# Twelve upward tile pairs by seven products, in groups of three, where ten stood in couples

## What is computed

```python
def conv_ffn(h, w_up, conv_w, w_down):
    gu = causal_dwconv(h @ w_up, conv_w)
    g, u = jnp.split(gu, 2, axis=-1)
    return (jax.nn.silu(g) * u) @ w_down
```

## Time and profile before

| | us |
|---|---|
| median of 3 runs | 1209.61 (1208.76 to 1210.14) |
| the profiled execution | 1209.19 |
| its span, first to last instruction | 1207.4 |

### The profile page before, as it was taken

How to read it: one execution, slowest core, us unless ns; L and a number is a source line. 1 busy time by engine, 2 the same in 40 slices (tenths; PEclk the granted TensorE clock), 3 DMA queues, 4 the chain that set the end, 5 groups by cost and what they waited for, 6 DMA issues and landing times.

```text
span 1207.4 us, 19455 instructions
## 1 busy us (share of the span) xinstructions
PE 1194.9 (99%) x7027; PEld 997.9 (83%) x7027; DVE 754.0 (62%) x1366; ACT 649.4 (54%) x1259; POOL 734.6 (61%) x566
## 2 busy tenths in 40 slices
PE   9999999999999999999999999999999999999997
PEld 7987777777888899988797777778999998898886
DVE  6655426756646777646597646436888886966224
ACT  6365535676645344455644666456666664333543
POOL 6773232353359776856384557548877776986842
PEclk9999999999999999999999999999999999999999
DMA  7332222122223333363242123343333334434332
GB/s 247 105 89 84 62 62 62 53 66 76 70 62 96 93 100 96 104 186 110 55 119 62 45 70 100 93 149 93 91 98 104 103 100 112 159 97 118 109 88 70
DMA packets 63016, 116.51 MB, mean 96 GB/s; under 512 B 6920, under 2 KB 11528, under 8 KB 62408
## 3 DMA queue, kind: packets, MB, share of 16 engines
q1 hardware_dynamic: 62776, 115.25, 33.1%
q10 hardware_dynamic: 144, 0.00, 0.0%
HBM read 110.97 MB, written 4.26 MB: 95 GB/s over the span
## 4 chain that ended last, share of the span: by engine, by line
PE 81%; DVE 11%; issue 3%; ACT 2%; POOL 1%; DMA 1%; SPq 0%; DVEq 0%; ACTq 0%; POOLq 0%
PE pb L1190 18%; PE pb L1191 18%; PE pb L1193 18%; PE pb L1252 3%; PE pb L1254 3%; PE pb L1253 3%; DVE t8s L2218 2%; PE pb L1408 2%; DVE cv L2125 2%; PE pb L1261 2%; PE pb L1384 2%; PE pb L1351 1%; PE pb L1322 1%; PE pb L1324 1%; PE pb L1323 1%
## 5 line engine op out<-in xcount | busy, mean ns | idle before, releaser
L2892 POOL TENSOR_TENSOR wlo<-raw,whi 128x512 fp32r<-128x512 f32 (+2 forms) x374 | 505.3, 1369 | 327.2 <-ACT whi L1617 323.1
L1190 PE MATMUL pb<-HH,whi 128*128 128x512 f32 x696 | 282.6, 406 | 0.0
L1617 ACT ACTIVATE whi<-raw 128x512 fp32r<-128x512 f32 (+3 forms) x373 | 221.4, 615 | 107.2 <-PE pb L1193 54.8
L1191 PE MATMUL pb<-HL,whi 128*128 128x512 f32 x696 | 275.3, 395 | 0.0
L1193 PE MATMUL pb<-HH,wlo 128*128 128x512 f32 x696 | 274.5, 394 | 0.0
L1190 PEld LDWEIGHTS pb<-HH,whi 128*128 128x128 f32 x696 | 131.1, 188 | 34.6 <-issue 4.6
L1191 PEld LDWEIGHTS pb<-HL,whi 128*128 128x128 f32 x696 | 131.0, 188 | 30.9 <-issue 2.9
L1193 PEld LDWEIGHTS pb<-HH,wlo 128*128 128x128 f32 x696 | 130.9, 188 | 30.5
L1758 ACT ACTIVATE P<-P,stat 128x256 f32<-128x256 f32 (+3 forms) x96 | 50.6, 527 | 78.5 <-DVE stat L2449 56.1
L2125 DVE SCALAR_TENSOR_TENSOR cv<-pb,vecs,cv 128x511 f32<-128x511 f32 x88 | 65.6, 745 | 2.4 <-ACT cv L2022 0.8
L2892 POOL TENSOR_TENSOR wlo<-s7a,whi 128x512 fp32r<-128x512 f32 x32 | 42.4, 1326 | 30.6 <-ACT whi L1617 30.4
(11 more groups left out here) (489 smaller groups left out, 2920.9 us busy)
## 6 DMA issues: line engine op xcount, KB each, us to landing
raw<-in_wall SPq DMA_DIRECT2D x368, 256.0 KB, 2.8
raw<-in_wall SPq DMA_DIRECT2D x8, 260.0 KB, 3.1
X<-in_xT SPq DMA_DIRECT2D x8, 256.0 KB, 5.6
X<-in_xT SPq DMA_DIRECT2D x2, 1024.0 KB, 8.4
x_kept<-X SPq DMA_DIRECT2D x2, 1024.0 KB, 6.5
X<-x_kept SPq DMA_DIRECT2D x2, 1024.0 KB, 6.1
outT<-PP SPq DMA_DIRECT2D x8, 256.0 KB, 2.6
raw<-in_wall SPq DMA_DIRECT2D x10, 192.0 KB, 2.4
```

Of the source, the lines that this page charges most:

```text
L1190: pe.do.matmul(b, hi, xh[k], start=start, stop=False, skip_group_check=tile[0] == "down")
L1191: pe.do.matmul(b, hi, xl[k], start=False, stop=False, skip_group_check=tile[0] == "down")
L1617: a.do.activation(whi[u % NS][:, 0:n], x, ACT.Copy).then_inc(*up("whi", ("whi", u)))
L2892: g.do.tensor_tensor(lo, x, hi.bitcast(F32), ALU.subtract).then_inc(*up(name, point))
```

## The change

One line: the table of tile pairs that go by seven products.

```diff
-UPS = (6, 7, 9, 10, 12, 13, 15, 16, 18, 19)
+UPS = (6, 7, 8, 10, 11, 12, 14, 15, 16, 18, 19, 20)
```

## The result

The changed kernel took 1213.06 us (median of 8 runs, 1212.63 to 1214.66), the kernel before beside it 1209.55 (8 runs, 1208.76 to 1210.47): a ratio of 1.0029, 95% interval 1.0019 to 1.004. The forecast was 1213.9, slower, with a range of 1211.4 to 1215.2. The profiled execution took 1213.06 us.

A forecast was written before the change was run, and what follows sets the result against it. A VectorE-ScalarE cycle of 11.66 us per seven-product pair, against TensorE's 9.81, was taken to bound grouped pairs. Four third pairs minus 42.34 us gave +4.3, added to the 1209.61 median: 1213.9 us, range 1211.4 to 1215.2.

The forecast's parts named there:

- The loop: Upward seven-product pairs: VectorE and ScalarE need 11.66 us from `u` to `u`, without waiting on TensorE, which needs 9.81.
- x: Time of a group's third seven-product pair, taken as 11.66 us; break-even at 10.59.
- The sum: Upward stage: four third pairs come, one couple-cycle and one plain pair go: 4 x 11.66 - 42.34 = +4.3 us.
- Where TensorE is held: Third pair of each group: TensorE waits 1.1 us at S2, then 0.7 us at A12, together 1.8 to 1.85.
- The name of the wait: Third pair: the profile shows TensorE waiting for VectorE's low half of S2 (line 2182), four times, about 1.1 us.
- No piling up: Between groups: one plain pair restores the old slack, about 1.6 us, so each group's first pair runs without a wait.
- Covers: Third pair and stage end: GpSimd's low halves, raw loads, banks and the single last plain pair cost nothing.
- A lag that doesn't grow: Rival: third pair held like the second, 1208.0 us (chance 0.04), or without any wait, 1206.5 (0.03); together 0.07.
- The 0.59 us: Rival: VectorE's idle time before `u` closes in the third pair, 11.07 us, +1.9 us, 1211.5; chance 0.08.
- The third pair waits for no load: Rival, opposite claim: third pair's loads or a GpSimd low half come 1 us late, +8.3 us, 1217.9; chance 0.07.

The follow-up runs named there:

- The two cuts into the loop: Changed kernel with ScalarE's copy of A11 one high half earlier: 1211.38 us; separately, changed kernel with sum S3 on GpSimd instead of VectorE: 1208.59 us.
- both edits: Changed kernel with ScalarE's copy of A11 one high half earlier and sum S3 on GpSimd instead of VectorE: 1206.46 us, ratio 0.9976.
- the last kernel: Changed kernel with ScalarE's copy earlier, S3 on GpSimd and the convolution's product one step later, at S4 instead of A12: 1205.11 us, ratio 0.9963.

## Why the prediction was right

- *The loop.* x = 11.66 was taken from `u` to `u` in couples. It held to 0.01 us in all eight places, with the same 0.59 us idle before `u`. The two cuts into the loop (0.26 and 0.60 us) moved the time by 1.7 and 4.5 us and the stage by 1.85 and 4.78, near 4 x 2 x 0.26 = 2.1 and 4 x 2 x 0.60 = 4.8.
- *The sum.* +4.3 us forecast, +3.82 in the stage, +3.9 in the span, +3.5 between medians. The term mis-sized is the stretch from a group's last `u` to the next group's first: 19.52 from the earlier trace rows was taken as fixed, and it is 19.44, 19.38 and 19.33, together 0.4 us less. TensorE comes through the plain pair and the start of the next group a little faster (the plain pairs take 11.17, 11.13 and 11.13 us by its starts, 11.18 or 11.19 before), and VectorE's wait at the end of the stretch is shorter (0.61, 0.55 and 0.50 us against 0.69); why was not followed.
- *Where TensorE is held.* Put at 1.1 us at S2 and 0.7 at A12 in the third pair; S2 came 878.72 - 874.59 = 4.13 us behind its pair's start instead of 2.81, 1.3 us late, and A12 883.35 - 878.72 = 4.63 us behind S2, where without a wait 933.51 + 0.12 - 929.48 = 4.15 lie between them, 0.5 us late. The sum, 1.8, is right. The shift from one to the other is mostly the hand-over of 0.15 us behind the low half, which the prediction left out. The low half itself ended 878.57 - 871.21 = 7.36 us behind `u`, as forecast.
- *The name of the wait.* Line 2182 was forecast, and the trace names ScalarE's `whi`. That is a coincidence of ends, as shown above; with S3's high half out of the way (S3 on GpSimd) VectorE's low half is named.
- *No piling up.* The first pair of each group runs without a wait, in 9.8 us; one plain pair is enough. At the end VectorE still waits 1.9 us for TensorE in the last plain pair (the L2113 row of the waits), as in the earlier trace rows, and the downward product starts 1025.51 - 1021.54 = 3.97 us later than before; the spans differ by the same 3.9.
- *Covers.* GpSimd's low half of the third pair's S4 ended at 883.58 (GpSimd's timeline), when TensorE had just begun A12 (883.35); no wait of TensorE names a transfer. Loads, GpSimd and banks cost nothing, as put.
- *The rivals.* A lag that doesn't grow (1208.0 or 1206.5) fell with the three `u`. The 0.59 us doesn't close by itself; where it was closed by hand, half of it came back elsewhere. The third pair waits for no load. By the rule of the Trainium skill, "Perfetto Trace Analysis", section "Identifying the Most-Contended Engine", TensorE was the one to relieve. The change took 177.59 - 176.46 = 1.1 us off the busy time of its products in the stage, and the kernel became slower: this case's trace disagrees. It is no clean test, since the busy time of the weight loads, by which the rule judges TensorE, rose from 161.58 to 163.59 us.

## What to carry to other kernels

Where an engine waits briefly and regularly for another that is not fully busy, measure the period of the step waited for against the engine's own: 11.66 against 9.81 us said at once how much each further piece of a longer run loses. Then read from the starts how much slack a run begins with: here 1.6 us, which the plain pair restores. Shorten the loop first (work to an idle engine, a copy out of a queue's back), then lengthen the groups: in the other order the same change lost 3.5 us. And when a wait is removed and the time stays, look at whether the period changed; if not, the wait has moved.

## What the runs showed of the hardware

A wait row names the semaphore that came last by the trace, and two ends 0.07 us apart (878.57 and 878.64) were enough to name the wrong engine in all four groups; TensorE's start 0.15 us behind an end was the better guide, three times over (878.57 to 878.72, 881.05 to 881.20, 881.09 to 881.24). The same sum of 128 x 512 takes 0.60 us from its start to the next step's on VectorE (877.29 to 877.89 in the kernel after, one operand in a bank) and 1.27 on GpSimd (874.21 to 875.48 with both edits, both operands in SBUF), and was still worth moving. In the last kernel `u` to `u` fell to 10.68, 0.12 less than with the same instructions in another order. VectorE's timelines, first of the kernel with both edits, then of that with the later product, show `u` to `u` and the place where they differ:

```profile
870.36 0.42 DVE L2303 TENSOR_TENSOR u<-pb,u 128x256 f32<-128x256 f32 x1
...
877.31 0.42 DVE L2303 TENSOR_TENSOR pb<-pb,w 128x256 f32<-128x256 f32 x1
877.77 0.70 DVE L2116 TENSOR_TENSOR pb<-pb,rff 128x512 f32<-128x512 f32 x1
...
881.17 0.42 DVE L2303 TENSOR_TENSOR u<-pb,u 128x256 f32<-128x256 f32 x1
```

```profile
870.44 0.42 DVE L2303 TENSOR_TENSOR u<-pb,u 128x256 f32<-128x256 f32 x1
...
876.05 0.42 DVE L2303 TENSOR_TENSOR pb<-pb,w 128x256 f32<-128x256 f32 x1
876.39 0.69 DVE L2128 SCALAR_TENSOR_TENSOR pb<-pb,cv 128x512 f32<-128x512 f32 x1
...
881.11 0.42 DVE L2303 TENSOR_TENSOR u<-pb,u 128x256 f32<-128x256 f32 x1
```

The same addition is followed after 0.46 us in the one and after 0.34 in the other. That an order alone is worth a tenth of a microsecond in each pair was not expected; the cause was not tried.
